# Hybrid block on one core: attention pairs spread over the mixer stage, softmax division on ScalarE, the mask folded into the bias, the residual scaling moved

## The reference, cut to what matters

```
h = modulate(rmsnorm_2(x, norm1_g[i]), sh1, sc1)
q, k, v, hv, hx1, hx2, gna, ghy = jnp.split(h @ w_in[i], IN_SPLITS, axis=-1)
# neighbourhood_attention, per head
s_nb = q_rot @ k_band * scale + bias
s_nb = jnp.where(col_ok[:, None, :], s_nb, NEG_INF)
s = jnp.concatenate([s_nb, s_ctx], axis=-1)
p = jax.nn.softmax(s, axis=-1)
o = p_nb @ v_band + p_ctx @ v_ctx
# hyena_mixer
u = short_conv(jnp.concatenate([hv, hx1, hx2], axis=-1), conv_w, conv_b)
for n in range(HY_ORDER):
    z = gates[n] * long_conv_bidir(z, filt[:, 0, n], filt[:, 1, n], bias[n])
# gated_merge and the residual
m = jax.nn.sigmoid(g_na) * (y_na @ w_na_o) + jax.nn.sigmoid(g_hy) * (y_hy @ w_hy_o)
x = x + g1 * (m @ w_out)
```

## Time and profile before

| what | us |
|---|---|
| median of 3 runs (lowest, highest) | 1020.57 (1018.99, 1021.89) |
| the profiled execution, its own time | 1020.99 |
| its span, first to last instruction | 1019.2 |
| PE busy in the span | 991.7 |
| DVE busy in the span | 803.5 |
| ACT busy in the span | 549.8 |

### The profile page before, as it was taken

How to read it: one execution, slowest core, us unless ns; L and a number is a source line. 1 busy time by engine, 2 the same in 40 slices (tenths; PEclk the granted TensorE clock), 3 DMA queues, 4 the chain that set the end, 5 groups by cost and what they waited for, 6 DMA issues and landing times.

```text
span 1019.2 us, 19818 instructions
## 1 busy us (share of the span) xinstructions
PE 991.7 (97%) x7928; PEld 961.6 (94%) x7928; DVE 803.5 (79%) x1425; ACT 549.8 (54%) x915; POOL 31.0 (3%) x36
## 2 busy tenths in 40 slices
PE   9999999999899999999999999789999999999997
PEld 5999999999799999999999998668999999999996
DVE  5888889975999789979887679999776787676553
ACT  5654444344777565564555357666444574545442
POOL 4000000000000000000000000100001100000000
PEclk9999999999999999999999999999999999999999
DMA  8666667984433258877686224242335565555541
GB/s 299 224 204 215 221 219 246 314 283 144 146 124 125 84 179 317 307 237 237 211 292 226 99 87 158 93 146 83 124 105 165 165 209 180 192 171 186 159 149 42
DMA packets 53717, 187.69 MB, mean 184 GB/s; under 512 B 6136, under 2 KB 7833, under 8 KB 53178
## 3 DMA queue, kind: packets, MB, share of 16 engines
q1 hardware_dynamic: 53450, 185.84, 55.1%
q10 hardware_dynamic: 176, 0.59, 0.1%
HBM read 185.36 MB, written 1.05 MB: 183 GB/s over the span
## 4 chain that ended last, share of the span: by engine, by line
PE 84%; DVE 10%; ACT 2%; issue 2%; DMA 1%; DVEq 0%; ACTq 0%
PE psum L436 83%; DVE memr L982 3%; DVE memr L1004 1%; PE psum L451 1%; ACT memr L1673 1%; DMA mem<-in_htok 1%; DVE psum L1432 1%; DVE mem L1440 0%; DMA mem<-in_w_up 0%; DVE mem L1414 0%; ACT mem L2003 0%; DVE mem L1416 0%; DVE mem L1014 0%; ACT memr L1684 0%; DVE mem L1249 0%
## 5 line engine op out<-in xcount | busy, mean ns | idle before, releaser
L436 PE MATMUL psum<-memr 128*128 128x256 f32 (+5 forms) x7652 | 955.6, 288 | 15.8 <-DVE memr L1004 7.5
L436 PEld LDWEIGHTS psum<-memr 128*128 128x128 f32 (+1 forms) x7652 | 930.0, 189 | 36.1 <-issue 20.3
L982 DVE TENSOR_TENSOR memr<-mem,memr 128x1024 fp32r<-128x1024 f32 (+1 forms) x290 | 337.8, 1199 | 56.4 <-ACT memr L1673 56.1
L1673 ACT ACTIVATE memr<-mem 128x1024 fp32r<-128x1024 f32 (+2 forms) x296 | 291.6, 1025 | 18.8 <-PE psum L436 9.0
L1684 ACT ACTIVATE memr<-mem 128x256 fp32r<-128x256 f32 (+4 forms) x171 | 81.5, 484 | 277.0 <-DVE mem L1114 104.3
L1004 DVE TENSOR_TENSOR memr<-mem,memr 128x256 fp32r<-128x256 f32 (+2 forms) x129 | 62.9, 495 | 13.3 <-ACT memr L1684 12.4
L1099 DVE TENSOR_TENSOR mem<-psum,mem 128x256 f32<-128x256 f32 (+1 forms) x66 | 27.9, 423 | 45.0 <-PE psum L436 45.0
L992 DVE CUSTOM_DVE_ANT_0 mem<-mem 128x1024 f32<-128x1024 f32 x48 | 58.5, 1219 | 0.6
L1681 ACT ACTIVATE mem<-mem 128x256 f32<-128x256 f32 (+1 forms) x56 | 22.8, 414 | 64.5 <-DVE mem L1640 31.9
L1004 DVE TENSOR_TENSOR memr<-psum,memr 128x256 fp32r<-128x256 f32 (+2 forms) x72 | 32.1, 462 | 7.8 <-ACT memr L1684 6.8
L1684 ACT ACTIVATE memr<-psum 128x256 fp32r<-128x256 f32 (+3 forms) x80 | 29.4, 401 | 15.2 <-PE psum L451 9.0
(11 more groups left out here) (132 smaller groups left out, 399.3 us busy)
## 6 DMA issues: line engine op xcount, KB each, us to landing
mem<-in_w_gate SPq DMA_DIRECT2D x66, 512.0 KB, 4.2
mem<-in_w_up SPq DMA_DIRECT2D x66, 512.0 KB, 4.5
mem<-in_w_ada SPq DMA_DIRECT2D x48, 512.0 KB, 4.5
mem<-in_w_down SPq DMA_DIRECT2D x48, 448.0 KB, 4.4
mem<-in_w_in SPq DMA_DIRECT2D x40, 512.0 KB, 3.9
mem<-in_w_down SPq DMA_DIRECT2D x24, 512.0 KB, 4.6
mem<-in_sb_qkv SPq DMA_DIRECT2D x24, 512.0 KB, 4.4
mem<-in_sb_o SPq DMA_DIRECT2D x8, 512.0 KB, 3.3
```

Source lines behind the costliest of these rows:

```text
L436: return pe.matmul(out, a, b, start=start, stop=stop)
L982: dve.tensor_tensor(r(ol, n), raw(e), rf(oh, n), ALU.subtract).then_inc(w_lo, 1)
L1673: act.activation(r(oh, n), raw(e), ACT.Copy).then_inc(w_hi, 1)
```

## The change

1. **Order of the attention.** MIX_TILES and the lists of PE, ACT and DVE are written anew. Values are computed between the keys and the attention steps rather than ahead of them, the first pair's scores come right after the last key, and the Hyena tiles that stood between the pairs give way to six gates. When the last pair's product is done, 5 Hyena tiles and 6 gates have been multiplied instead of 8 and 1. The first gates (EARLY = 6) are copied out of PSUM raw, and their sigmoid is taken in two wide operations behind the last pair (`early_gates`).
2. **Mask.** The mask is written into the bias table on the host (`np.where(inside, ..., NEG)`). The table `na_mask`, its DMA, its 384 columns and POOL's eight additions go.
3. **Division on ScalarE.** DVE takes only the reciprocals (`softmax_sums`); the multiplication of the probabilities is an ACT copy with a per-row scale (`softmax_scale`). The four reductions of a pair now follow each other.
4. **Residual scaling.** Its eight DVE operations move from between the key tiles to behind `used(26)`, which follows `transform(0)`.

```
-MIX_TILES = ("q0 h0 h1 q1 h2 h3 h4 q2 h5 q3 h6 g0 h7 h8 h9 g1 h10 h11 g2 g3 g4 g5 g6 g7 g8 g9 g10 g11 g12 g13 g14 "
+MIX_TILES = ("q0 q1 h0 h1 g0 q2 g1 h2 g2 q3 g3 h3 h4 g4 g5 h5 h6 h7 h8 h9 g6 h10 h11 g7 g8 g9 g10 g11 g12 g13 g14 "
...
+        def softmax_sums(p):
+            for qb in range(2):
                 for h in range(2):
-                    x, c = 2 * h + qb, 8 * p + 4 * qb + 2 * h
-                    total = f(STAT + 2 * x + 1, 1)
+                    total = f(STAT + 2 * (2 * h + qb) + 1, 1)
                     dve.wait_ge(ns_exp, 4 * p + 2 * qb + h + 1)
-                    dve.reciprocal(total, total).then_inc(ns_norm, 1)
-                    dve.wait_ge(ns_norm, c + 1)
-                    dve.tensor_scalar(f(PX[x], 512), f(PX[x], 512), total, None, ALU.mult, ALU.bypass).then_inc(ns_norm, 1)
+                    dve.reciprocal(total, total).then_inc(ns_sum, 1)
...
+        def softmax_scale(p):
+            for qb in range(2):
+                for h in range(2):
+                    x = 2 * h + qb
+                    act.wait_ge(ns_sum, 4 * p + 2 * qb + h + 1)
+                    copy(f(PX[x], 512), f(PX[x], 512), f(STAT + 2 * x + 1, 1)).then_inc(ns_norm, 1)
```

PE's list from the first key tile on, the part between the first and third pair's attention:

```
         k_mm(0)
         v_rows(3, TMP[1])
         k_mm(1)
+        q5(0)
         k_mm(2)
+        v_mm(0)
         k_mm(3)
-        q5(0)
-        v_mm(0)
...
+        na_attend(0)
+        na_scores(1)
+        h_rows(0)
+        h_mm(1)
+        g_mm(0)
+        v_rows(7, TMP[1])
+        q5(2)
+        na_turn(1)
+        g_mm(1)
+        na_attend(1)
+        na_scores(2)
+        h_rows(1)
+        h_mm(2)
+        g_mm(2)
+        q5(3)
+        na_turn(2)
+        g_mm(3)
+        na_attend(2)
+        na_scores(3)
+        h_rows(2)
+        h_mm(3)
+        h_mm(4)
+        h_rows(3)
+        g_mm(4)
+        na_turn(3)
+        g_mm(5)
+        h_rows(4)
         na_attend(3)
...
         filter_tile(0)
-        h_mm(8)
-        h_mm(9)
-        g_mm(1)
-        h_rows(7)
+        h_mm(5)
+        h_mm(6)
+        h_mm(7)
+        h_rows(5)
         pe.wait_ge(table_lo, 2)
         spectrum(0)
```

ACT's list around the second pair (DVE's has the same order, with `softmax_sums(1)` behind `h_conv(1)`), and the scaling's new place on DVE:

```
+        softmax(1)
+        h_rows(0)
+        h_step(1)
+        softmax_scale(1)
+        used(4)
+        gate(0)
         v_rows_high(7)
+        used(5)
+        q_step(2)
+        q_turned(2)
+        used(6)
+        weights_high(1)
+        gate(1)
+        na_high(1)
+        softmax(2)
...
         matrix_low(0)
         filter_tile(0)
+        h_conv(5)
+        h_conv(6)
+        used(18)
...
+        used(23)
         transform(0)
         used(26)
+        for i in range(KT):
+            dve.scalar_tensor_tensor(hx(i, NMETA, T1), hx(i, NMETA, T1), vec("final_norm", i), f(SROOT, T1),
+                                     ALU.mult, ALU.mult)
         dve.wait_ge(x1_cp, 4)
```

More of the change, by code:

```diff
@@ L93, in neighbour_bias @@
     cq, ck = np.arange(64)[:, None], np.arange(64)[None, :]
-    halves = [wide[:, 5 - half:11 - half][:, :, ck - cq + 63] for half in (0, 1)]
+    start = np.clip(cq - 8, 0, 48)
+    inside = (ck >= start) & (ck < start + 16)
+    halves = [np.where(inside, wide[:, 5 - half:11 - half][:, :, ck - cq + 63], np.float32(NEG)) for half in (0, 1)]
     return np.ascontiguousarray(np.concatenate([x.transpose(0, 2, 1, 3) for x in halves], axis=1).reshape(8, 128, 384))
-MIX_TILES = ("q0 h0 h1 q1 h2 h3 h4 q2 h5 q3 h6 g0 h7 h8 h9 g1 h10 h11 g2 g3 g4 g5 g6 g7 g8 g9 g10 g11 g12 g13 g14 "
+MIX_TILES = ("q0 q1 h0 h1 g0 q2 g1 h2 g2 q3 g3 h3 h4 g4 g5 h5 h6 h7 h8 h9 g6 h10 h11 g7 g8 g9 g10 g11 g12 g13 g14 "
              "g15").split()
+KV_ORDER = (0, 1, 2, 4, 3, 5, 6, 7)
+EARLY = 6
 W_POOL = 0
@@ L287, in build @@
     QN, QR = ([z5.take(T1) for _ in range(2)] for _ in range(2))
-    NB, NMASK = [z5.take(768) for _ in range(2)], z5.take(384)
+    NB = [z5.take(768) for _ in range(2)]
     z5.at = max(z5.at, FREE_SC + 7 * 1024)
@@ L877, in tensor @@
         filter_tile(1)
+        h_rows(6)
+        h_mm(8)
+        h_rows(7)
+        h_mm(9)
+        g_mm(6)
+        spectrum(1)
         h_mm(10)
         h_mm(11)
[L880 to L884, removed]
         pe.wait_ge(table_lo, 3)
@@ L887, in tensor @@
         transform(0)
-        for m in range(6, 10):
+        for m in range(7, 10):
             g_mm(m)
@@ L2044, in scalar @@
+        k_turned(1)
+        q_step(0)
+        q_turned(0)
+        k_step(2)
+        k_turned(2)
+        v_step(0)
+        high_halves(W_MIX + 2)
+        k_step(3)
+        v_rows_high(4)
+        k_turned(3)
+        softmax(0)
+        v_step(1)
+        high_halves(W_MIX + 3)
+        softmax_scale(0)
+        q_step(1)
+        v_rows_high(5)
+        q_turned(1)
+        v_step(2)
+        high_halves(W_MIX + 4)
+        weights_high(0)
         h_step(0)
+        v_rows_high(6)
+        v_step(3)
@@ L2056, in scalar @@
-        used(5)
-        weights_high(0)
+        softmax_scale(2)
+        gate(2)
+        used(9)
+        q_step(3)
+        q_turned(3)
+        used(10)
+        weights_high(2)
+        gate(3)
+        used(11)
+        na_high(2)
+        softmax(3)
+        h_rows(2)
         h_step(3)
-        used(6)
-        h_rows(2)
+        softmax_scale(3)
+        used(12)
         h_step(4)
-        used(7)
         h_rows(3)
-        h_rows(4)
-        q_step(2)
-        used(8)
-        softmax(1)
@@ L2091, in scalar @@
         copy(r(W3S, 2048, 0, 64), f(W3R, 2048, 0, 64)).then_inc(table_hi, 1)
+        gate(5)
+        h_rows(4)
+        used(15)
         na_high(3)
@@ L2127, in scalar @@
         matrix_high(0)
+        early_gates()
         filter_tile(0)
+        h_step(5)
+        h_step(6)
+        used(18)
+        h_rows(5)
+        h_step(7)
+        spectrum(0)
+        h_rows(6)
+        filter_tile(1)
         h_step(8)
-        used(14)
+        h_rows(7)
         h_step(9)
-        used(15)
-        h_rows(7)
-        gate(1)
-        used(16)
-        spectrum(0)
-        filter_tile(1)
-        h_step(10)
-        used(17)
-        h_step(11)
-        used(18)
-        gate(2)
-        used(19)
-        gate(3)
-        used(20)
+        gate(6)
+        used(21)
         spectrum(1)
         matrix_high(1)
-        gate(4)
-        used(21)
-        gate(5)
-        used(22)
+        h_step(10)
+        h_step(11)
+        used(23)
         transform(0)
-        for m in range(6, 10):
+        for m in range(7, 10):
             gate(m)
```

274 lines of the change are left out of this document (107 added, 167 removed).

## The result

The changed kernel takes **1032.60 us** (median of 4 runs, 1030.56 to 1034.95), the kernel before beside it 1020.22 (4 runs). The ratio is **1.0124, 95% interval 1.0109 to 1.0139**: slower by 12.4 us. The forecast had the direction, but its loss of 5.8 is about half of the 12.4, and 1032.6 lies above the range's end of 1030. The profiled execution after is the fastest of its four, 1030.56 (span 1028.7, mean granted clock 0.990; the others 0.986, 0.985, 0.986; the runs of before that the experiments list had 0.988 to 0.996). So the trace shows 9.6 of the 12.4 us against the trace of before (1020.99).

The account below looks back on a forecast made before the run. PE was taken to bound the kernel almost everywhere, with DVE's list between 613 and 695.88 us. List losses of 2.0 plus 3.8 for the clock made 5.8 us more: 1026.4 us, range 1014.5 to 1030.

Parts of the forecast that it names:

- q0: First query tile, now right after k1: PE waits 2.3 us for its split and low half, a wait hidden before.
- `na_attend(1)`: Pair 1's attention product: PE idles 5.3 us ahead of it, until the first low half of the probabilities.
- `na_attend(2)`: Pair 2's attention product: PE idles 4.1 us ahead of it.
- `h_rows(5)`: Behind the filters' start, PE waits 2.9 us for h5's convolution, behind DVE's whole filter tile; 1.11 before.
- the back-transform: Two tile splits between h11 and DVE's transform(0), covered by three products instead of four: 0.2 us lost.
- `transform(1)`: Scaling behind used(26) delays the back-transform products: 3.3 us of PE idle where there was none.
- The division on ACT: Each ACT division of the probabilities was taken at 0.61 us, bounds 0.49 and 0.69.
- The first pair's scores: First reduction at 603.8 against 615.80 before, with 0.7 us booked separately as won from the mask.
- The first rival: Busy time decides, not the lists: the attention idle times and their clock loss vanish, 1013.2 us; chance 0.25.
- The clock: Half clock behind the idle times ahead of pairs 1 and 2's attention products: 1.9 us each, 3.8 together.
- The third rival: Clock falls also at q0's wait, spectrum(0) and transform(1), up to 1.7 us each: about 1030; chance 0.13.
- the walk of a pair: Reductions to next pair's: 20.2, 21.9, 21.9 us, then 18.7 to the filter table; PE's last group 0.7, output halves 1.7.

Follow-up runs that it names:

- e6: The kernel before with only the division moved to ACT, in the old order: 1020.09 us, ratio 0.9999.
- e7: The kernel before with only the eight residual scalings moved behind used(26): 1021.90 us, ratio 1.0018.
- e9: The changed kernel with the sixteen divisions back on DVE, each behind its reciprocal: 1028.76 us, ratio 1.0076 to the kernel before.
- e1: The changed kernel with unread filler matmuls on PE ahead of pairs 1 and 2's attention products and transform(1): 1026.80 us, ratio 1.0063 to the kernel before.
- e5: The kernel before with only the mask moved into the host's bias table, POOL's eight additions gone: 1016.58 us, ratio 0.9957.
- e4: The changed kernel with pairs 1 and 2's probability halves ahead of the next query's steps on ACT and DVE: 1025.28 us, ratio 1.0050 to before.
- e8: The changed kernel with scaling in the merge, q0 behind k2, probabilities ahead of the query's steps, h_rows(5) behind spectrum(0): 1017.45 us, ratio 0.9974 to before.
- e2: The changed kernel with the eight scalings moved from behind used(26) into the merge loop: 1027.96 us, ratio 1.0070 to the kernel before.

## Why the prediction came out as it did

**What held.** The losses were placed where they came and nearly at their size: q0 2.25 (2.3), `na_attend(1)` 5.18 (5.3), `na_attend(2)` 3.98 (4.1), `h_rows(5)` 2.52 (2.9), the back-transform 0.24 (0.2), `transform(1)` 2.79 (3.3). The division on ACT is 0.61 to 0.62 (0.61). From the filters to `transform(1)` it takes 66.23; the forecast's own sums give 66.9 (from 685.8 to 2.0 behind 750.7).

One hit is in part luck. The first pair's scores are reduced at 603.23 (603.1), and 0.7 of that was booked as won from the mask ahead of the first value transposes. They do come 0.93 earlier, and 0.87 of it is the shorter wait there, but e6 and e7 wait only 0.45 with POOL's additions in place: the trace of before happened to have an addition on top of a DVE operation that PE waited for.

The first rival, busy time decides, is refuted by e6 and e9, not only by the result: work taken from the saturated engine gave nothing in the old order and cost 3.8 in the new one. The Trainium skill (Perfetto Trace Analysis, "Optimizing Scalar/DVE Operations") says that where DVE is saturated, moving some work to ScalarE may make sense. In the runs here it did not.

**The step that failed is "The clock".** It took 1.9 for each of two falls, 3.8, and gave the rest (q0, `spectrum(0)`, `transform(1)`) to a rival of 0.13. Four things were wrong with it.
- The fall behind `transform(1)`'s wait is in the trace (0.79 in 760 to 764): the stretch from there to the landmark that I compare, the four f32 matmuls of 256 columns behind the mixer, takes 83.37, against 81.81 in e1 and 81.7 before. That is 1.6 to 1.7 which the forecast left out. The two falls that it did price were dearer in it than in the rows: 1.66 and 1.32.
- It took the trace of one execution for the kernel. Behind one and the same idle time of 2.20 the clock fell before and not in e5; at 2.73 ahead of the product that follows the exponentials it stayed up before (3.07) and fell in e6:

```profile
641.23 4.50 PE L437 MATMUL psum<-memr 128*128 128x256 f32 x24 [2.73 <-ACT mem L2002]
```

- It counted one fall in the trace of before, and there is a second one, in code that the change does not touch. PE's timeline before (the first row) and after (the second), behind the same wait:

```profile
264.15 2.69 PE L436 MATMUL psum<-memr 128*128 128x512 f32 x7 [3.29 <-DVE memr L1188]
...
264.74 1.57 PE L441 MATMUL psum<-memr 128*128 128x512 f32 x7 [3.28 <-DVE memr L1197]
```

  The granted clock in 264 to 268 is 0.59 in the one and 1.00 in the other. Of the 13 traces here, four show these seven matmuls at 2.68 or 2.69, two in between (1.86, 2.27) and seven at 1.57.
- So a short wait has a chance of a fall, not a yes or a no, and a kernel with five such waits more has a clock that differs from run to run. The executions after show 0.985 to 0.990; the profiled one, with the best clock, was 2.0 below the median, while the profiled one of before was 0.4 above it. The forecast subtracted 0.4 where 2.0 were to be added. The third rival was the nearer one, and it too was too small by its own prices: three falls at 1.7 on top of 1026.4 make 1031.5 and not 1030.

The fill of e1 takes three falls away: 4.5 by rows, 5.8 by medians. The Trainium skill (TensorE: Matmul & The Clock Gate, "What's actually happening") lets the array fall after being idle for a while. The idle times of 5.18 and 3.98 agree with it. Of the ones between 1.8 and 3.3 some are followed by a fall and some are not: 1.87 in e4 is (24 matmuls in 4.60) and 1.88 in e8 is not (3.08). So by itself it does not tell which.

**The second error is in the walk of a pair.** e1 shows the pairs without falls: first reductions at 602.97, 623.70, 646.45, 669.36 and filters at 688.39, that is 20.7, 22.75, 22.9 and 19.0, where the walk gave 20.2, 21.9, 21.9, 18.7. Together 2.7 too little. In the two middle pairs the step is the last one, "PE's last group 0.7" behind low halves that trail: PE's twelve matmuls start at 18.0 of the pair (17.7 in the walk) and take 3.05 in one piece, so the output halves on ACT and DVE can start only at 21.05 and not at 20.2. The smaller waits behind it (0.4 and 0.5 less than forecast) give some of this back.

**The account of the 6.2 us** between 1026.4 and 1032.6, in the traces: the walk 2.1 (the landmark of e1 stands 4.15 behind that of before, forecast 2.0), the clock 1.1 more than 3.8 in the profiled execution (e1 to after, 4.9 at the landmark, of which 0.25 is there at the first value transposes), 0.5 at the last matmuls of the span, and 2.5 between the profiled execution and the medians. The 0.5 is no loss of the change: e4 and e8 end as before does, 186.86 behind the landmark, and others 187.4.

The 2.5 is the largest. No slower execution of the changed kernel itself was traced, but e2's trace (1029.87, clock 0.987) has the same lists up to `transform(0)` and shows two places where falls come and go. Its filters start at 695.28, against 691.75 in the changed kernel's trace. Of these 3.5, 1.7 are there at 557 us, ahead of the stage (558.69 against 556.99 for the same f32 products), where the one fall on record is that behind the wait at 261 (2.69 for seven matmuls, as before), and 1.55 come behind q0's wait:

```profile
589.98 13.03 PE L441 MATMUL psum<-memr 128*128 128x256 f32 x96 [2.25 <-DVE memr L991]
```

The changed kernel's trace has 11.48 for these 96, behind the same 2.25 (588.25 above). With e9's fall at `h_rows(5)`, each of the three places of the third rival shows a fall in some trace. How often each comes in the changed kernel is not measured.

**By parts,** each alone on the kernel before: the mask -3.2, the division none to +0.3, the scaling +2.1. They add up to about -1, and all together cost +12.4. The new order must be the rest, about 13, but it was not tried alone, and the parts do not simply add: the same division costs 0.3 at most there and 3.8 here, the same scaling 2.1 and 4.6. The order itself is not bad: with q0, the probabilities, `h_rows(5)` and the scaling moved, and the division left on DVE, it makes the fastest kernel here. What it lacks are a few positions in the lists where an instruction that somebody waits for stands behind one that nobody needs yet.

## What to carry to other kernels

Where each engine works through a fixed list, do not ask how busy an engine is, but what stands in front of the instruction that the other engine waits for; moving work from a full engine to an emptier one can lengthen the hand-over by more than it frees, and a run with the work moved alone tells it. Move the instruction that somebody waits for ahead of the one that nobody needs, and price a PE wait with the half clock behind it (here 1.2 to 1.7 us for a full fall, behind waits between 1.87 and 5.18), as a chance over several runs rather than from one trace. Products that nobody reads, put into the waits, show how much of a loss is the clock's. Compare two traces from the start of the changed stage on: code that both share can differ by a fall.

## What was not expected of the hardware

- Useless matmuls in three waits made the kernel 5.8 us faster (1032.60 to 1026.80), and the spread of its runs fell from 4.4 to 1.3.
- The same idle time of 2.20 ahead of the same twelve matmuls was followed by 4.58 in one kernel and 3.03 in another; 2.73 and 2.74 ahead of the same 24 matmuls by 3.07, 3.04 and 4.50; 3.28 and 3.29, in code that all kernels here share, ahead of the same seven by 1.57, 1.86, 2.27 and 2.69.
- Eight additions of 384 columns on POOL, some 9 us of its time (2.17 for two) in a stage where it has nothing else to do, cost the kernel 3.2 us by what they delay on DVE: a DVE operation of 256 columns took 1.23 beside one of them and takes 0.41 to 0.43 in e5.
